# The joined norm and column projection of a hybrid decoder layer on one core: four reorderings within the engines' queues

## The reference, cut to what matters

```python
xn = rmsnorm(x, norm_pre)                  # (2080, 1024)
parts = split_cols(xn @ w_in)              # 9296 columns
# a_q, a_k: short causal convolution, then SiLU, before the mLSTM branch
y = b + w[0] * up[:, 0:T]
for j in range(1, CONV_W): y = y + w[j] * up[:, j:j + T]
qk = silu(y)
# b_q, b_k, b_iq: columns of the sparse attention; b_ik, b_iw, a_i, a_f: small columns
# sample rows: top 256 of 8196 positions by index score, per row
_, sel = lax.top_k(indexer_scores(iq, iw, ik_all, visible), 256)
```

## Time and profile before

| | us |
|---|---|
| median of 3 runs (4315.5 to 4335.87) | 4315.9 |
| profiled execution | 4316.0 |
| its span, first to last instruction | 4314.4 |
| PE busy | 4062.0 |
| VectorE busy | 2738.9 |
| ScalarE busy | 1391.0 |
| POOL busy | 1371.5 |
| mean granted clock of PE | 0.976 |

### The profile page before, as it was taken

The page is one execution under the profiler, slowest core; times in us unless marked ns, Lnnn a source line. Parts: engine busy times, 40 slices in busy tenths (PEclk is TensorE's granted clock), DMA queues, the critical chain, the costliest instruction groups (busy, mean ns, idle before and its releaser), DMA issues. The chain is left out here.

```text
span 4314.4 us, 38829 instructions
## 1 busy us (share of the span) xinstructions
PE 4062.0 (94%) x13646; PEld 2149.2 (50%) x13646; DVE 2738.9 (63%) x3657; ACT 1391.0 (32%) x2499; POOL 1371.5 (32%) x1256
## 2 busy tenths in 40 slices
PE   7799989999999999999998799889998999999999
PEld 4455545564445555545554565545553455544444
DVE  3479999629999999999993555544443222243333
ACT  3411211143243333333221665544443322101111
POOL 0000025532255565555553222122101343352111
PEclk9899999999999999999999899999998999999999
DMA  5211212330111111121112543222122644441111
GB/s 205 74 53 55 76 61 77 105 132 34 50 57 66 53 59 58 65 70 58 68 60 83 168 109 87 63 66 80 47 89 71 210 140 144 133 173 49 59 54 43
DMA packets 294574, 367.16 MB, mean 85 GB/s; under 512 B 43044, under 2 KB 244664, under 8 KB 291691
## 3 DMA queue, kind: packets, MB, share of 16 engines
q1 hardware_dynamic: 253742, 248.07, 18.7%
q0 software_dynamic: 21728, 95.93, 6.0%
q10 hardware_dynamic: 18912, 20.72, 1.7%
HBM read 235.11 MB, written 128.23 MB: 84 GB/s over the span
## 5 line engine op out<-in xcount | busy, mean ns | idle before, releaser
L1121 DVE MAX8 best<-score 128x8 f32<-128x2048 f32 (+13 forms) x448 | 639.5, 1427 | 89.8 <-POOL score L1090 74.9
L1123 DVE MATCH_REPLACE8 score<-best,score 128x2048 f32<-128x2048 f32 (+13 forms) x448 | 631.1, 1409 | 0.0
L372 PE MATMUL pg<-xnT,wt 128*128 128x416 f32 x800 | 284.7, 519 | 7.1 <-ACT u L497 7.1
L1475 PE MATMUL mix_slot<-mix_kT,mix_bq 128*128 128x512 f32 (+3 forms) x640 | 267.3, 549 | 4.5 <-DVE mix_mx L1731 3.6
L1051 POOL TENSOR_TENSOR kT<-kT 128x416 f32<-128x416 f32 x160 | 171.1, 1070 | 281.8 <-ACT kT L1011 278.2
L1495 PE MATMUL mix_po<-mix_probT,mix_v 128*128 128x512 f32 x544 | 239.8, 594 | 0.9 <-ACT mix_probT L1607 0.9
L3035 PE MATMUL out_u<-early,out_w 128*128 128x416 f32 x640 | 230.4, 517 | 8.5 <-PEq L73 8.5
L945 PE MATMUL pr<-xnT,w_row 128*128 128x416 f32 x640 | 235.2, 514 | 0.0
L1731 DVE CUSTOM_DVE_ANT_0 early<-mix_slot,mix_mk 128x1024 f32<-128x1024 f32 (+7 forms) x86 | 84.8, 986 | 230.0 <-PE mix_slot L1475 228.6
L3035 PE MATMUL out_u<-out_yT,out_w 128*128 128x416 f32 x640 | 224.3, 512 | 0.0
L372 PEld LDWEIGHTS pg<-xnT,wt 128*128 128x128 f32 x800 | 153.8, 193 | 136.5 <-issue 128.5
(11 more groups left out here) (586 smaller groups left out, 7544.7 us busy)
## 6 DMA issues: line engine op xcount, KB each, us to landing
gt_scr<-kT SPq DMA_DIRECT2D x40, 832.0 KB, 3.6
out_gm<-gt_scr ACTq DMA_DIRECT2D x80, 208.0 KB, 2.8
w0a<-in_w_in SPq DMA_DIRECT2D x12, 1024.0 KB, 5.3
wt<-in_w_in SPq DMA_DIRECT2D x22, 512.0 KB, 4.3
w_row<-in_w_in SPq DMA_DIRECT2D x10, 1024.0 KB
qt_scr<-kT POOLq DMA_DIRECT2D x8, 1040.0 KB, 4.9
qt_scr<-u POOLq DMA_DIRECT2D x10, 832.0 KB
gt_scr<-kT SPq DMA_DIRECT2D x20, 416.0 KB
```

Source lines behind the costliest of these rows:

```text
L372: ins = nc.tensor.matmul(pg[0:m, g, 0:GW], w[:, k, 0:m], c["xnT"][:, k, g * GW:(g + 1) * GW], start=k == 0, stop=k == KT - 1)
L1121: nc.vector.max(best[:, :], sc).then_inc(top_step, 1)
L1123: nc.vector.match_replace(sc, best[:, :], sc, TAKEN).then_inc(top_step, 1)
L1475: ins = mm(slot[:, s, a:a + m], bq[p][:, hd, :], kT[:, hd // 4, lo + a:lo + a + m], start=True, stop=True)
```

## The change

Four orders change; no instruction is added or taken away.

1. In `first_products()` a product carries the number of a tile that is turned in its middle (after four of its eight steps), and some tiles are turned ahead of products as before. ScalarE gives the statistics three tiles ahead of such a tile before it waits for the product.
2. SP loads the third pair (pair 2) ahead of `move_candidates`.
3. ScalarE does `copies(n)` ahead of `sigmoid(n - 1)` for n from 3 to 7; `sigmoid(7)` comes last.
4. VectorE makes the second token sums at the start of step 22 of the 32 merge steps, in place of after the merge.

```diff
--- before.py
+++ after.py
@@ -110,11 +110,11 @@
 
 def first_products():
 
+    turns = {(0, 0): ((), 4), (1, 0): ((5,), 6), (0, 1): ((7,), 8), (1, 1): ((), 9), (0, 2): ((10,), 11),
+             (1, 2): ((), 12), (0, 3): ((13,), 14), (1, 3): ((15,), 16), (0, 4): ((), None), (1, 4): ((), None)}
     return [("norm", n) for n in range(4)] + [
-        ("prod", 0, 0), ("norm", 4), ("prod", 1, 0), ("norm", 5), ("norm", 6), ("prod", 0, 1), ("norm", 7),
-        ("prod", 1, 1), ("norm", 8), ("norm", 9), ("prod", 0, 2), ("norm", 10), ("prod", 1, 2), ("norm", 11),
-        ("norm", 12), ("prod", 0, 3), ("norm", 13), ("prod", 1, 3), ("norm", 14), ("norm", 15), ("norm", 16),
-        ("prod", 0, 4), ("prod", 1, 4)]
+        e for (n, g), (before, inside) in turns.items()
+        for e in [("norm", t) for t in before] + [("prod", n, g, inside)]]
 
 
 def transposed_projection_phase(nc, c, d):
@@ -196,7 +196,7 @@
         x_turned, xnT_out, halo_t = sem("x_turned"), sem("xnT_out"), sem("halo_turned")
         halo_out = sem("halo_out")
         starts = first_products()
-        first_number = {e: i for i, e in enumerate(e for e in starts if e[0] == "prod")}
+        first_number = {e[1:3]: i for i, e in enumerate(e for e in starts if e[0] == "prod")}
 
         w_in = d["w_in"].rearrange("a (k p) n -> (a p) k n", p=P)
         block = ctx.enter_context(nc.Block())
@@ -275,8 +275,9 @@
                          c["sm"][:, 0:NB, 0:ID]).then_inc(sm_stored, 16)
             sp.dma_start(d["o_ik_sample"].rearrange("a b t e -> (a b t) e"), c["sm"][0:SR, NB, 0:ID]).then_inc(sm_stored, 16)
             load_pair(1)
+            load_pair(2)
             move_candidates(sp)
-            for x in range(2, ITEMS):
+            for x in range(3, ITEMS):
                 load_pair(x)
             sp.wait_ge(gate_stored, 32)
             sp.wait_ge(m_stored, 16)
@@ -399,8 +400,8 @@
                 if kind == "norm":
                     turn(n)
                     continue
-                g, = group
-                v = first_number[kind, n, g]
+                g, inside = group
+                v = first_number[n, g]
                 if g == 0:
                     pe.wait_ge(w_loaded[n], 16)
                 pe.wait_ge(xnT_out, 2 * min(NT, -(-(g + 1) * GW // P)))
@@ -409,6 +410,8 @@
                 if v >= G:
                     pe.wait_ge(group_out, v - G + 1)
                 for k in range(KT):
+                    if k == KT // 2 and inside is not None:
+                        turn(inside)
                     ins = nc.tensor.matmul(pg[:, v % G, 0:GW], wt[n][:, k, :], c["xnT"][:, k, g * GW:(g + 1) * GW],
                                            start=k == 0, stop=k == KT - 1)
                 ins.then_inc(group_mm, 1)
@@ -517,17 +520,19 @@
                     if n + LEAD < NT:
                         statistics(n + LEAD)
                     continue
-                g, = group
-                v = first_number[kind, n, g]
+                g, inside = group
+                if inside is not None and inside + LEAD < NT:
+                    statistics(inside + LEAD)
+                v = first_number[n, g]
                 act.wait_ge(group_mm, v + 1)
                 nc.scalar.copy(u[n][:, 3 + g * GW:3 + (g + 1) * GW], pg[:, v % G, 0:GW]).then_inc(group_out, 1)
             sigmoid(0)
             copies(2)
             sigmoid(1)
-            sigmoid(2)
             for n in range(3, NCONV):
                 copies(n)
-                sigmoid(n)
+                sigmoid(n - 1)
+            sigmoid(NCONV - 1)
             act.wait_ge(stored[0], 16 * NP_CONV)
             for g in range(G):
                 at = slice(g * GW, (g + 1) * GW)
@@ -612,7 +617,7 @@
             def tile(j, p, conv, warm):
                 n = 2 * j + p
                 a, raw, us = acc[p], u[p], c["us"]
-                dve.wait_ge(group_out, G * (n + 1) if n else first_number["prod", 0, G - 1] + 1)
+                dve.wait_ge(group_out, G * (n + 1) if n else first_number[0, G - 1] + 1)
                 if warm:
                     dve.wait_ge(stored[p], 16 * j)
                 av = a[:, SEQ:ROWS].rearrange("p (b t) -> p b t", t=DT)
@@ -703,8 +708,7 @@
             dve.wait_ge(m_stored, 16)
             token_terms(0)
             take(dve, range(2 * NCONV + 10, TOPK // 8))
-            finish_take(dve)
-            token_terms(1)
+            finish_take(dve, 22, lambda: token_terms(1))
             finish_places(dve)
             keep(dve)
 
@@ -2247,7 +2251,7 @@
             nc.vector.max_index(idx[:, 8 * j:8 * j + 8], v8, score[:, :])
             link(nc.vector.match_replace(score[:, :], v8, score[:, :], TAKEN))
 
-    def finish(dve):
+    def finish(dve, middle, between):
         place = idx[:, :].bitcast(I32)
         nc.vector.tensor_scalar(pint[:, 0, :], place, 7, None, ALU.arith_shift_right)
         link(nc.vector.tensor_scalar(pint[:, 1, :], place, PAGE - 1, None, ALU.bitwise_and))
@@ -2265,6 +2269,8 @@
         dve.wait_ge(moved, 16 * 8)
         flat = val4[:, :, :].rearrange("p s k -> p (s k)")
         for j in range(TOPK // 8):
+            if j == middle:
+                between()
             link(nc.vector.max(best[:, :], flat))
             link(nc.vector.match_replace(flat, best[:, :], flat, TAKEN))
         link(nc.vector.scalar_tensor_tensor(flat, flat, TAKEN, idf4[:, :, :].rearrange("p s k -> p (s k)"),
```

## The result

The changed kernel takes 4281.69 us (median of 7 runs, 4272.37 to 4288.52) against 4314.66 us (7 runs). The medians are 33.0 us apart. The ratio of the runs is 0.9916, with a 95% interval of 0.9897 to 0.9935: 0.8% faster, clear of no change. The forecast was 4283.5 us in a range of 4272 to 4299. The profiled execution took 4281.08 us, its span is 4279.5 us, 34.9 us less than before.

What follows compares the result with a forecast made beforehand. The prediction took PE, busy 94%, to bound the kernel. Its terms 12.3 - 0.4 + 13.1 + 7.5 = 32.5 us, off 4316.0 us, gave 4283.5 us, range 4272 to 4299.

Steps and rivals of the forecast that it cites:

- What bounds: Whole program: PE, busy 94%, sets the time, and PE still comes last at the barrier, by 9 us over VectorE.
- Part 1: Turned tiles inside the first products: column waits and slow clock go, gaining 12.3 us, bounds 6.5 to 12.9.
- Part 2: Sigmoids after the next copies: PE's wait moves to the tile after the small weights, net -0.4 us, bounds -2.2 to +8.9.
- Part 3: Third pair's weights loaded earlier: the whole stall ahead of item 2 goes, gaining 13.1 us, lower bound 9.
- Part 4: Second token sums at merge step 22: item 5's stall and its slow clock go, gaining 7.5 us, lower bound 3.
- The slack of VectorE: End of the phase: VectorE's chain ends at 828, PE at 836.9; VectorE slip over 9 us is all lost.
- (a): First products: transposes inside keep the clock low; 4328 us, slower, chance 0.03; mild form 4295 to 4300, chance 0.06.
- (b): Small tile: PE is not held at 451.6 because ScalarE reaches its copies sooner; 4274 us, chance 0.05.
- (c): VectorE becomes the bound through late copies or longer waits in the sums; 20 us of slip gives 4294, chance 0.07.
- (d): Second token sums: moving them only trades the wait, since POOL and VectorE still collide; 4287 to 4291 us, chance 0.10.
- (e): Item 2: the early weights do nothing because something else, such as the sums, holds it; 4292 to 4297 us, chance 0.04.

Runs made afterwards that it cites:

- the one with the gates' bank read earlier: Changed kernel with small copies ahead of sigmoid(7) and VectorE reading the gates' bank behind five top-k rounds, not six; 4288.82 us, ratio 0.9927 to the kernel before.

## Why the prediction was right, point by point

- **What bounds.** PE, in every stretch that the change touches. Right: each gain of PE up to the barrier arrived in the span, and the rest of the program took 3445.9 us against 3446.1.
- **Part 1, 12.3 us forecast, 13.8 measured, of which 1.3 varies with the execution.** From the turn of tile 5 (179.79) to the copy at 235.13 it is 55.34 us, against 55.2 reckoned, and the clock was 1.00. The 1.3 us on top lie ahead of that, where I had put both orders equal: the first product and the turn of tile 4 took 8.19 us (171.60 to 179.79) against 9.52 (173.07 to 182.59), because the slow clock at the start of the phase ended sooner (a granted clock of 0.80 over this stretch, against 0.68 before). That varies with the execution: in seven of the ten other kernels with the new order the first half product took 5.88 or 5.89 us, not some 4.7, and this stretch then takes 9.53 us, as in the old order. By item 0 only 0.4 us of the difference is left. So by such an execution part 1 gains 12.5 us and part 2 neither gains nor loses. The row is from the kernel with part 3 undone:

```profile
173.49 5.89 PE L414 MATMUL pg<-xnT,wt 128*128 128x416 f32 x8 [2.08 <-DVE xnT L600]
```

- **Part 2, -0.4 forecast, -0.9 measured**; undoing it gained 0.3 us. The wait moved as described: 7.60 us on ScalarE's third small copy, reckoned 7.5. The clock afterwards cost 2.1 us (58.13 against 56.03), reckoned 1.75.
- **Part 3, 13.1 forecast, 13.3 measured** in the difference of the profiles (11.7 of waiting and 1.6 of clock), 14.9 when it alone is undone.
- **Part 4, 7.5 forecast, 7.0 measured.** I had put POOL half a microsecond ahead of PE there, and it came half a microsecond late: its last weight sum ends at 705.35, and PE, after 0.50 us of waiting, goes on at 705.44. VectorE waited 4.09 and 1.15 us there, as forecast (4, then 1 to 2), and its sums took 1.89 to 2.75 us. The sum of parts holds only for the four together. Singly undone, the parts cost 13.5, -0.3, 14.9 and 15.9, which is 44 us and not 33.2.
- **The slack of VectorE** was the step that failed, and it cost nothing here. I put it at 9 us and wrote that every further microsecond would be lost. Its last wait was 11.9 us: on the old scale (15.3 us later) its chain ended at 827.2, 828 was reckoned, and PE was done at 838.2, 836.9 was reckoned. And the run with the sums at step 12 shows that up to the barrier it is some 18 us, since POOL's last stores, as far as the rows show, cover more. I had read the barrier as released by PE, since PE's last work was the last to release another engine, and had not asked what the 9.80 us between that work and the next phase were. (PE's last work in the kernel before begins at 857.6 us, and does not end there as I wrote; VectorE goes on at 858.53.)
- **The rivals.** (a) is out: the clock stayed at 1.00 from 179.80 on, with twelve single turns (tiles 5 to 16) in and between products. The rule of the Trainium skill, "TensorE: Matmul & The Clock Gate", Part 4 (PE-mode transpose), that transposes do not count as busy work like matmuls, fits with the slow products behind two turns and 2 us of waiting (two times of three in the kernel with part 1 undone), and single turns of 0.87 us did no harm. Whether the turns or the waiting brought the clock down, no run here separates. (b) is out, with the new wait in the profile. (c) did not occur, and its price was overstated: of 25.7 us of slip 7.5 were lost. Of (d) a remainder of 0.5 us was there. (e) is out: item 2 started 25.14 us after item 1.

The whole came to 34.9 us in the profiled execution against 32.5. Of the 2.4 us between, 1.5 lie ahead of the phase, where the two kernels do the same, and 1.5 in part 1; the other parts take 0.8 of it back, and the rest gives 0.2.

## What to carry to other kernels

Ask of a wait that an edit removes not only how long it is but which chain paces the engine behind it. VectorE's convolution, at 27.78 us a tile, set when the small tile could be copied, so 7 us won in one place were waited for some 130 us later, and became a gain of 7.5 us only when three further orders were changed as well. Undo parts in pairs, too: two fixes in series on one engine can each look worth 15 us and together be worth 20. And read a slack up to the barrier, not up to the last busy engine: here the barrier opened 9.8 us behind PE's last work, most likely because stores were in flight, and VectorE's lateness cost nothing until it reached that point.

## What the runs showed of the hardware that was not expected

The same instructions behind this phase took 3439.9 to 3469.5 us in the profiled executions. Much of the difference lies in one stretch. PE's busy time from 3000 to 3400 us and the granted clock (the figure behind it) in the kernel with part 4 undone, then in the one with the gates' bank read earlier, which had the shortest and the longest rest:

```profile
3000.00:3400.00 400.00, 360.51 (x1368) 0.95 0.34 105
```

```profile
3000.00:3400.00 400.00, 362.57 (x1265) 0.86 0.31 96
```

The clock is 0.95 in one and 0.86 in the other, over nearly the same instructions (1368 and 1265 of them got done). By an estimate from these rows, 0.09 of 400 us is 36 us of full clock, or 32 over the 360 us in which PE was busy, and the two rests differ by 29.6. The other profiled executions lie between, in nearly the same order by this clock as by their rest (0.91 with 3454.1 us, 0.92 with 3452.4, 0.93 with 3445.9 to 3450.7, 0.94 with 3442.6 to 3448.0). What decides the clock there was not settled. An effect of a few microseconds is read here from a stretch of the timeline, not from whole runs.
